# Retention in a two-layer diffusion backbone: rotated queries loaded in three groups instead of chunk by chunk

## The chip, the cores and the metric

The kernel runs on one core of a Trainium2 chip. The metric is the device time of one execution in microseconds (us). Engines are named as the profile names them: PE is TensorE (matmuls), PEld its weight loads, DVE is VectorE, ACT is ScalarE, POOL is GpSimd, SP is the SyncE queue, which issues every load and store spoken of here. All data is float32.

## The reference, cut to what matters

Two layers work on 1024 latent tokens behind 256 context tokens, width 1024. Each layer projects its tokens into three groups of heads (retention, latent attention, grouped attention), joins their outputs in one projection and ends with a gated MLP. The change lies in retention: 6 heads of 64, chunks of 128 tokens, both directions.

```python
def retention_scan(q, k, v, log_gamma, state0):          # chunks of c = 128 tokens
    scores = jnp.einsum('bhncd,bhnsd->bhncs', qc, kc) * decay_mask[None, :, None]
    intra = jnp.einsum('bhncs,bhnse->bhnce', scores, vc)
    kv = jnp.einsum('bhnsd,bhnse->bhnde', kc * k_decay[None, :, None, :, None], vc)
    def step(state, kv_n):
        return chunk_decay[None, :, None, None] * state + kv_n, state
    _, states_prev = lax.scan(step, state0.astype(dt), jnp.moveaxis(kv, 2, 0))
    cross = jnp.einsum('bhncd,nbhde->bhnce', qc * q_decay[None, :, None, :, None], states_prev)
    return (intra + cross).reshape(b, h, t, dv)

def bidir_retention(q, k, v, log_decay, state_fwd, state_bwd):
    out_f = retention_scan(q, k, v, log_decay[0], state_fwd)
    out_b = flip_t(retention_scan(flip_t(q), flip_t(k), flip_t(v), log_decay[1], state_bwd))
    return out_f + out_b

def retention_out(o, g, gn_w):                           # per head: centre, divide by the root of the variance, gate
    ...
```

`q` here is the query after the axial rotation. The product `qc * q_decay` is made on the chip for both directions; it is the tile `qd` below.

## The kernel before, in words

A layer runs one stage after another: input projection, retention, attention, output projection, MLP. The stages are blocks with no overlap between them. The order of the work on each engine is written out by hand, and semaphores carry the waits between engines. The input projection leaves rotated queries, keys, values and gates of retention in a scratch tensor in HBM (`proj`); keys and values are also kept on the chip.

The function `retention` (L1051) has two parts.

**State part.** For each of the 10 chunks PE turns keys and values to token order (`to_tokens`, L1155 and L1162), ACT copies them into `kz` and `vz`, DVE makes the decayed values `vd` from `vz` (L1318), PE multiplies `kz` and `vd` into one state increment (L1176) and counts it in `kv_done`. ACT keeps the increment, DVE scans the states (`scan`, L1325 and L1327). `kz` and `vd` have two slots each and nobody reads them after the last increment, `kv_done` = 10. During this part SP loads the zero-padded queries `qz` (L1111), the first two chunks of `rq` and `gate` (L1115, L1116), and the first head of the attention stage (`fetch_head`, L766 to L769). `rq` holds the same rotated queries as `qz`, unpadded, in two slots of one chunk.

**Chunk loop.** It runs over the chunks of `order`: 10 in the first layer, 8 (without the context) in the last. In iteration i PE does, in this order, `inner(i)` (keys times queries, L1188), `variance(i - 2)` (L1214), `outer(i - 1)` (12 matmuls: L1203 masked scores times values, L1206 `qd` times state), `spread(i - 2)` (L1222). Two more iterations without an `inner` end it. DVE does `masked(i)` (L1352), `invert(i - 2)` (L1358, L1361), one step of the backward scan, `finish(i - 2)` (L1366, L1371), which counts `out_done`. ACT does the roots, the square of the output (L1283) and the block diagonal state (L1276). POOL makes `qd` for both directions, two products of 128x384 for each chunk (L1146), and is busy with nothing else in the loop.

The waits that bear on the change:

```python
pe.wait_ge(at_done, i + 1)       # outer(i): masked scores of chunk i
pe.wait_ge(bd_done, 2 * (i + 1)) #           diagonal states of chunk i
pe.wait_ge(qd_done, 2 * (i + 1)) #           decayed queries of chunk i
if i >= 2: pe.wait_ge(out_done, i - 1)   #   finish(i - 2) has read the output bank
```

On POOL, `qd(i)` waits for the load of `rq(i)` and, from chunk 2 on, for `outer(i - 2)` (`main_done`), which has read the slot of `qd`. On SP, the loads of `rq(i + 2)` and `gate(i + 2)` wait for `out_done` of chunk i, that is for `finish(i)`, and for `qd(i)`; the store of chunk i follows them.

Of the kernel before, what the change touches and what calls it, by code (L numbers as in the profile page):

```python
# [14 lines left out]
P = 128  # L15
KB = D // P
BLK = TOK // P
# [10 lines left out]
T_RK, T_RV, T_RQ, T_RG = (x - RK for x in (RK, RV, RQ, RG))  # L28
# [21 lines left out]
def backbone(nc, a):  # L50
    f32, f32r = mybir.dt.float32, mybir.dt.float32r
    ALU, ACT, AX = mybir.AluOpType, mybir.ActivationFunctionType, mybir.AxisListType
# [4 lines left out]
    def scratch(name, shape):  # L57
        return nc.dram_tensor(f"{name}_scratch", shape, f32, kind="Internal").ap()
    proj = scratch("proj", (NTILE - RK, P, TOK))
# [702 lines left out]
    def fetch_head(sp, h, q0, q1, q2, k1, k2, sem):  # L762

        rows = slice((h % 2) * HD, (h % 2 + 1) * HD)
        for part, q, k in ((0, q1, k1), (1, q2, k2)):
            sp.dma_start(k[:HD, :].bitcast(f32), mk_d[part, h // 2, rows, :]).then_inc(sem, 16)  # L766
            sp.dma_start(k[HD:MD, :].bitcast(f32), kr_d[part]).then_inc(sem, 16)
            sp.dma_start(q[:HD, q0:].bitcast(f32), mq_d[part, h // 2, rows, q0:]).then_inc(sem, 16)
            sp.dma_start(q[HD:MD, q0:].bitcast(f32), mq_d[part, 2, h * MR:(h + 1) * MR, q0:]).then_inc(sem, 16)  # L769
# [281 lines left out]
    def retention(layer, last, first_head):  # L1051
        W = RH * HD
        back = list(range(XB - 1, -1, -1)) + list(range(BLK - 1, XB - 1, -1))
        order = back[XB:] if last else back
        NO = len(order)
        q0 = CTX if last else 0
        with Scope() as s:
# [3 lines left out]
            cdec = s.sb("cdec", [P, 3, 2])  # L1061
            decq = s.sb("decq", [P, 2, 3, P])
            mask, mtmp = s.sb("mask", [P, RH, P]), s.sb("mtmp", [P, RH, P])
            rq, gate = s.sb("rq", [P, 2, 3, P]), s.sb("gate", [P, 2, 3, P])
            qz = s.sb("qz", [P, 3, 2, TOK])
            kz = s.sb("kz", [P, 2, 3, 2 * P])
            vz = s.sb("vz", [P, BLK, 3, 2 * P])
            vd = s.sb("vd", [P, 2, 3, 2, 2, HD])
            kv = s.sb("kv", [P, BLK, 3, 2, HD])
            state = s.sb("state", [P, BLK, 3, 2, HD])  # L1070
            bd = s.sb("bd", [P, 2, 3, 2, P])
            qd = s.sb("qd", [P, 2, 2, 3, P])
# [7 lines left out]
            pa = [s.ps(f"pa{i}", [P, 1024]) for i in range(2)]  # L1080
            po = psum_banks(s, "po", 2)
            mats_in, qz_in, head_in = s.sem("mats_in"), s.sem("qz_in"), s.sem("head_in")
            rq_in = [s.sem(f"rq_in{k}") for k in range(2)]
            gate_in = [s.sem(f"gate_in{k}") for k in range(2)]
            kz_zero, vz_zero, bd_zero, qz_zero = s.sem("kz_zero"), s.sem("vz_zero"), s.sem("bd_zero"), s.sem("qz_zero")
            arg, dec_made, masks_made, mask_made, decq_made = (s.sem(x) for x in ("arg", "dec_made", "masks_made", "mask_made", "decq_made"))
# [1 line left out]
            vd_done, kv_done, kv_kept = s.sem("vd_done"), s.sem("kv_done"), s.sem("kv_kept")  # L1088
            own, fwd_done, bwd_done = s.sem("own"), s.sem("fwd_done"), s.sem("bwd_done")
            a_done, at_done, main_done, bd_done, qd_done = (s.sem(x) for x in ("a_done", "at_done", "main_done", "bd_done", "qd_done"))  # L1090
# [2 lines left out]
            out_stored = [s.sem(f"out_stored{k}") for k in range(2)]  # L1093
            block = s.enter_context(nc.Block())
            halves = [slice(0, HD), slice(HD, P)]

            def own_columns(x, half):

                return x[:, :, half * (P + HD):half * (P + HD) + HD]
# [4 lines left out]
            @block.sync  # L1104
            def _(sp):
                sp.dma_start(centre[:, :], a["ret_centre"]).then_inc(mats_in, 16)
                sp.dma_start(og[:, :], a["ones_gqa"]).then_inc(mats_in, 16)
                c0 = q0
                sp.wait_ge(qz_zero, 2)
                for half in range(2):  # L1110
                    sp.dma_start(qz[halves[half], :, half, c0:], proj[T_RQ:T_RQ + 3, halves[half], c0:].rearrange("t p n -> p t n")).then_inc(qz_in, 16)  # L1111

                def load_chunk(i):
                    c = order[i]
                    sp.dma_start(rq[:, i % 2, :, :], proj[T_RQ:T_RQ + 3, :, c * P:(c + 1) * P].rearrange("t p n -> p t n")).then_inc(rq_in[i % 2], 16)  # L1115
                    sp.dma_start(gate[:, i % 2, :, :], proj[T_RG:T_RG + 3, :, c * P:(c + 1) * P].rearrange("t p n -> p t n")).then_inc(gate_in[i % 2], 16)  # L1116
                load_chunk(0)
                load_chunk(1)
                fetch_head(sp, 0, q0, *first_head, head_in)
                for i, c in enumerate(order):  # L1120
                    sp.wait_ge(out_done, i + 1)
                    if i + 2 < NO:
                        sp.wait_ge(qd_done, 2 * (i + 1))
                        load_chunk(i + 2)
                    sp.dma_start(mix[O_RET:O_RET + 3, :, c * P:(c + 1) * P].rearrange("t p n -> p t n"),
                                 tout[:, i % 2, :].rearrange("p (t n) -> p t n", t=3)).then_inc(out_stored[i % 2], 16)
                for k in range(2):
                    sp.wait_ge(out_stored[k], 16 * (NO // 2))
                sp.wait_ge(head_in, 128)

            @block.gpsimd
            def _(pool):
                nc.gpsimd.memset(kz[:, :, :, HD:P + HD], 0.0).then_inc(kz_zero, 1)
                for half in range(2):
                    pool.wait_ge(qz_zero if half else kz_zero, 1)
                    nc.gpsimd.memset(qz[halves[1 - half], :, half, :], 0.0).then_inc(qz_zero, 1)
                pool.wait_ge(qz_zero, 2)
                nc.gpsimd.memset(vz[:, :, :, HD:P + HD], 0.0).then_inc(vz_zero, 1)
                nc.gpsimd.memset(bd[:, :, :, :, :], 0.0).then_inc(bd_zero, 1)
                pool.wait_ge(decq_made, 6)  # L1140
                for i, c in enumerate(order):
                    pool.wait_ge(rq_in[i % 2], 16 * (i // 2 + 1))
                    if i >= 2:
                        pool.wait_ge(main_done, i - 1)
                    for d in range(2):
                        nc.gpsimd.tensor_tensor(qd[:, i % 2, d, :, :], rq[:, i % 2, :, :], decq[:, d, :, :], ALU.mult).then_inc(qd_done, 1)  # L1146

            @block.tensor
            def _(pe):
# [602 lines left out]
    with main:  # L1752
        first_modulations()
        clear_semaphores()
        for layer in range(DEPTH):
            last = layer == DEPTH - 1
            input_projection(layer, last)
            with Scope() as s:
                first_head = [s.sb(x, [P, TOK], f32r) for x in ("first_qh", "first_ql", "first_kh", "first_kl")]
                retention(layer, last, first_head)  # L1760
                attention(layer, last, first_head)
            output_projection(layer, last)
            mlp(layer, last)

            clear_semaphores()
        final_norm()
# [111 lines left out]
```

## Time and profile before

The median of three runs is 3946.09 us (3945.66 to 3949.57). The profiled execution spans 3941.5 us from its first to its last instruction; the profile gives no other time of that execution.

| | |
|---|---|
| span of the profiled execution | 3941.5 us |
| mean granted TensorE clock | 0.956 |
| PE busy | 3540.9 us, 90% |
| DVE busy | 2487.8 us, 63% |
| ACT busy | 1250.1 us, 32% |
| POOL busy | 669.9 us, 17% |
| HBM traffic | 77 GB/s over the span |
| retention, first layer | from 489.5 to 632.2 us of the span |
| retention, last layer | up to 2652.9 us |

Busy time is the time in which an engine executes; a wait is not busy. The granted clock is a share of TensorE's full speed: 1.00 is its upper level, 2.4 GHz, and 0.50 its lower level, 1.2 GHz. A timeline row gives start, duration, engine, line, operation, output and inputs, how many instructions it merges, and in brackets how long the engine stood idle before it and what released it. A float32 matmul stands as two instructions in these counts, so the 12 matmuls of `outer` are 24.

### The profile page before, as it was taken

The numbers are of one execution on the slowest core, as the hardware profiler recorded it, in microseconds if no ns is written. First come the engines' busy times: TensorE is split into PE (matmuls) and PEld (weight loads), VectorE is DVE, ScalarE is ACT, GpSimd is POOL, SyncE is SP. The second block draws the span as 40 slices with busy tenths as digits, with TensorE's granted clock in tenths as the row PEclk, the third lists the DMA queues.
The fourth block names the chain that finished last, engine by engine and source line by source line (L and its number), as shares of the span: only waits on it lengthen the run. The fifth ranks groups of instructions, "written<-read, shape, count | busy, mean of one in ns | idle before, by whom it ended". The sixth has DMA issues, their size and how long they took to land. (4 is left out here: it accounts for less than half of the span.)

```text
span 3941.5 us, 49189 instructions
## 1 busy us (share of the span) xinstructions
PE 3540.9 (90%) x18524; PEld 2974.4 (75%) x18524; DVE 2487.8 (63%) x3355; ACT 1250.1 (32%) x2126; POOL 669.9 (17%) x284
## 2 busy tenths in 40 slices
PE   2899977999698999999998899869997799999996
PEld 2687776888576888888887577769996577777774
DVE  5655544677427999998866523437784366666666
ACT  1432133667313112111121432316673222222222
POOL 0111120000111222232221111210001132222331
PEclk9899988999899999999999899979998899999998
DMA  5235335121201122112110323424112111111111
GB/s 189 93 120 194 146 78 169 41 50 38 102 19 59 64 77 82 64 65 90 43 33 16 119 94 135 153 66 140 47 36 91 33 48 38 42 48 48 48 48 43
DMA packets 97226, 306.58 MB, mean 78 GB/s; under 512 B 11840, under 2 KB 40384, under 8 KB 95296
## 3 DMA queue, kind: packets, MB, share of 16 engines
q1 hardware_dynamic: 97088, 304.69, 23.6%
q8 instruction: 93, 1.52, 0.2%
q14 instruction: 45, 0.37, 0.0%
HBM read 240.29 MB, written 64.36 MB: 77 GB/s over the span
## 5 line engine op out<-in xcount | busy, mean ns | idle before, releaser
L117 POOL TENSOR_TENSOR wlo<-raw,whi 128x1024 fp32r<-128x1024 f32 x190 | 490.0, 2596 | 1787.1 <-ACT whi L106 1787.0
L145 PE MATMUL up_acc<-h_hi,whi 128*128 128x512 f32 (+1 forms) x1760 | 654.7, 372 | 37.6 <-POOL wlo L117 18.6
L1672 DVE SCALAR_TENSOR_TENSOR xT<-down_acc,mod,xT 128x512 f32<-128x512 f32 (+1 forms) x880 | 562.2, 696 | 177.6 <-PE down_acc L147 174.7
L146 PE MATMUL up_acc<-h_lo,whi 128*128 128x512 f32 (+1 forms) x1760 | 649.9, 369 | 0.0
L147 PE MATMUL up_acc<-h_hi,wlo 128*128 128x512 f32 (+1 forms) x1760 | 649.3, 369 | 0.0
L106 ACT ACTIVATE whi<-raw 128x1024 fp32r<-128x1024 f32 x190 | 200.0, 1056 | 763.6 <-PE down_acc L147 351.0
L145 PEld LDWEIGHTS up_acc<-h_hi,whi 128*128 128x128 f32 x1760 | 333.1, 189 | 103.6 <-ACT up L1599 45.3
L147 PEld LDWEIGHTS up_acc<-h_hi,wlo 128*128 128x128 f32 x1760 | 332.8, 189 | 56.3
L146 PEld LDWEIGHTS up_acc<-h_lo,whi 128*128 128x128 f32 x1760 | 333.2, 189 | 54.2 <-issue 0.2
L145 PE MATMUL proj_acc<-h_hi,whi 128*128 128x512 f32 (+1 forms) x920 | 343.0, 373 | 28.3 <-DVE h_lo L353 15.5
L145 PE MATMUL down_acc<-hid_hi,whi 128*128 128x512 f32 (+1 forms) x880 | 333.1, 379 | 19.9 <-POOL hid_lo L1525 19.9
L1011 DVE TENSOR_REDUCE negmax<-scores 128x1 f32<-128x1280 f32 (+1 forms) x180 | 247.0, 1372 | 162.0 <-PE scores L902 162.0
L146 PE MATMUL proj_acc<-h_lo,whi 128*128 128x512 f32 (+1 forms) x920 | 336.7, 366 | 0.0
L147 PE MATMUL proj_acc<-h_hi,wlo 128*128 128x512 f32 (+1 forms) x920 | 336.3, 366 | 0.0
L147 PE MATMUL down_acc<-hid_hi,wlo 128*128 128x512 f32 (+1 forms) x880 | 330.5, 376 | 0.0
L146 PE MATMUL down_acc<-hid_lo,whi 128*128 128x512 f32 (+1 forms) x880 | 328.7, 374 | 0.0
L206 DVE SCALAR_TENSOR_TENSOR mod_acc<-norm_buf,cs,mod_acc 128x384 f32<-128x384 f32 x364 | 325.8, 965 | 0.7 <-DVE xT L707 0.7
L1525 POOL TENSOR_TENSOR hid_lo<-y,hid_hi 128x1281 fp32r<-128x1281 f32 (+1 forms) x44 | 120.4, 2737 | 1175.0 <-ACT hid_hi L1610 1175.0
L1599 ACT ACTIVATE up<-up_acc 128x512 f32<-128x512 f32 (+1 forms) x220 | 119.4, 550 | 563.2 <-PE up_acc L147 562.9
L980 ACT ACTIVATE pth<-scores 128x512 fp32r<-128x512 f32 (+1 forms) x500 | 225.9, 522 | 211.9 <-PE scores L912 211.9
L1025 DVE TENSOR_TENSOR ptl<-scores,pth 128x512 fp32r<-128x512 f32 (+1 forms) x500 | 264.9, 583 | 13.7 <-ACT pth L980 13.7
L1651 DVE TENSOR_SCALAR y<-up,convw 128x1281 f32<-128x1281 f32 (+1 forms) x88 | 122.7, 1394 | 203.8 <-ACT up L1599 203.8
(191 smaller groups left out, 5916.4 us busy)
## 6 DMA issues: line engine op xcount, KB each, us to landing
raw<-in_w_mlp SPq DMA_DIRECT2D x132, 512.0 KB, 3.9
norm_buf<-in_w_ada SPq DMA_DIRECT2D x52, 768.0 KB, 4.7
raw<-in_w_proj SPq DMA_DIRECT2D x42, 512.0 KB, 5.7
proj_scratch<-stage SPq DMA_DIRECT2D x18, 640.0 KB, 3.6
xT<-in_xT SPq DMA_DIRECT2D x2, 5120.0 KB, 27.0
ada_raw<-in_w_ada SPq DMA_DIRECT2D x12, 768.0 KB, 4.5
raw<-in_w_mix SPq DMA_DIRECT2D x16, 512.0 KB, 6.2
xT<-proj_scratch SPq DMA_DIRECT2D x4, 1920.0 KB, 8.6
```

The lines of the kernel that those rows point to most:

```text
L106: nc.scalar.activation(self.hi[k][:, :], self.raw[k][:, :], ACT.Copy).then_inc(self.hi_ready, 1)
L117: nc.gpsimd.tensor_tensor(self.lo[k][:, :], self.raw[k][:, :], self.hi[k][:, :].bitcast(f32), ALU.subtract).then_inc(self.lo_ready, 1)
L145: nc.tensor.matmul(out, hi, xhi, start=start, stop=False)
L146: nc.tensor.matmul(out, hi, xlo, start=False, stop=False)
L147: return nc.tensor.matmul(out, lo, xhi, start=False, stop=stop)
L206: ins = nc.vector.scalar_tensor_tensor(at, self.raw[:, kb, :], cs[:, kb, w:w + 1], at, ALU.mult, ALU.add)
L980: nc.scalar.activation(pth[G % 2][:, k0:k1, j * P:(j + 1) * P], S[n % 2][:, k0 * P:k1 * P].rearrange("p (b q) -> p b q", q=P), ACT.Copy).t ...
L1011: nc.vector.tensor_reduce(negmax[:, n:n + 1], S[n % 2][:, :CTX if is_ctx(n) else TOK], AX.X, ALU.max, negate=True).then_inc(max_done, 1)
L1025: nc.vector.tensor_tensor(ptl[G % 2][:, k0:k1, j * P:(j + 1) * P], S[n % 2][:, k0 * P:k1 * P].rearrange("p (b q) -> p b q", q=P), pth[G % ...
L1525: nc.gpsimd.tensor_tensor(hid_lo[:, lo_col:hi_col], y[1][:, lo_col:hi_col], hid_hi[:, lo_col:hi_col].bitcast(f32), ALU.subtract).then_inc( ...
L1651: nc.vector.tensor_scalar(o, u[:, lo_col:hi_col], cw(1), cw(3), ALU.mult, ALU.add).then_inc(tap, 1)
L1672: nc.vector.scalar_tensor_tensor(xs, db[g % DB][:, :w], mod_of(layer, 5, m, c), xs, ALU.mult, ALU.add).then_inc(added, 1)
```

## The change: what it does

The two-slot tile `rq` is gone. The chunks of `order` are split into three groups of 2, 4 and 4 (in the last layer 2, 4 and 2), each of them one run of adjacent columns, and each is loaded by one DMA. The first group has a tile of its own, `rq_first`, of the size that `rq` had. The second goes into the memory of `kz`, the third into the memory of `vd`. SP issues the loads of groups two and three after `fetch_head`, as soon as `kv_done` is 10. In the loop SP loads only the gate of chunk i + 2 after `out_done` of chunk i, and no longer waits for `qd_done` there. POOL waits for the semaphore of the chunk's group and reads the chunk's columns from it; its wait for `main_done` stays.

```diff
-            rq, gate = s.sb("rq", [P, 2, 3, P]), s.sb("gate", [P, 2, 3, P])
+            gate = s.sb("gate", [P, 2, 3, P])
+            rq_first = s.sb("rq_first", [P, 3, 2 * P])
...
+            rq_more = [kz[...] as [P, 3, 512], vd[...] as [P, 3, 512]]
...
+            groups = [(rq_first, order[0:2]), (rq_more[0], order[2:6]), (rq_more[1], order[6:10])]
+            def group_of(i):
+                return 0 if i < 2 else 1 if i < 6 else 2
+            def queries(i):
+                dst, cs_ = groups[group_of(i)]
+                at_ = (order[i] - cs_[-1]) * P
+                return dst[:, :, at_:at_ + P]
...
-                def load_chunk(i):
+                def load_queries(g):
+                    dst, cs_ = groups[g]
+                    sp.dma_start(dst[:, :, :len(cs_) * P],
+                                 proj[T_RQ:T_RQ + 3, :, cs_[-1] * P:(cs_[0] + 1) * P].rearrange("t p n -> p t n")).then_inc(rq_in[g], 16)
+                def load_gate(i):
                     c = order[i]
-                    sp.dma_start(rq[:, i % 2, :, :], proj[T_RQ:T_RQ + 3, :, c * P:(c + 1) * P].rearrange("t p n -> p t n")).then_inc(rq_in[i % 2], 16)
                     sp.dma_start(gate[:, i % 2, :, :], ...)
-                load_chunk(0)
-                load_chunk(1)
+                load_queries(0)
+                load_gate(0)
+                load_gate(1)
                 fetch_head(sp, 0, q0, *first_head, head_in)
+                sp.wait_ge(kv_done, BLK)
+                load_queries(1)
+                load_queries(2)
                 for i, c in enumerate(order):
                     sp.wait_ge(out_done, i + 1)
                     if i + 2 < NO:
-                        sp.wait_ge(qd_done, 2 * (i + 1))
-                        load_chunk(i + 2)
+                        load_gate(i + 2)
...
-                    pool.wait_ge(rq_in[i % 2], 16 * (i // 2 + 1))
+                    pool.wait_ge(rq_in[group_of(i)], 16)
...
-                        nc.gpsimd.tensor_tensor(qd[:, i % 2, d, :, :], rq[:, i % 2, :, :], decq[:, d, :, :], ALU.mult).then_inc(qd_done, 1)
+                        nc.gpsimd.tensor_tensor(qd[:, i % 2, d, :, :], queries(i), decq[:, d, :, :], ALU.mult).then_inc(qd_done, 1)
```

## Rows read from the trace of the kernel before

**Rows 1.** Instructions of tile `qd`, whole program: durations in ns, idle and waits.

```profile
L1146 POOL TENSOR_TENSOR qd<-rq,decq x36: 991/991/1703, 515.9 to 2640.6; 128x384 f32<-128x384 f32 x36
...
  DMA rq<-proj_scratch: 151.5, 14
...
  PE po L1203: 62.4, 14
```

**Rows 2.** Timeline of the first layer's loop, iteration 3: the load and what follows.

```profile
536.23 0.38 SPq L1115 DMA_DIRECT2D rq<-proj_scratch  x1
...
538.96 1.94 POOL L1146 TENSOR_TENSOR qd<-rq,decq 128x384 f32<-128x384 f32 x2 [18.02 <-DMA rq<-proj_scratch]
...
541.16 1.19 PE L1203 MATMUL po<-at,vz 128*128 128x128 f32 x4 [4.36 <-POOL qd L1146]
```

**Rows 3.** Timeline of iteration 2 and of the start of iteration 3.

```profile
529.80 1.46 PE L1188 MATMUL pa<-qz,xT 128*128 128x256 f32 x6
...
531.69 0.69 PE L1203 MATMUL po<-at,vz 128*128 128x128 f32 x4
...
534.45 0.49 PE L1222 MATMUL pv<-ident,wide 128*128 128x128 f32 x3
...
534.77 1.46 PE L1188 MATMUL pa<-qz,xT 128*128 128x256 f32 x6
...
535.05 0.56 DVE L1366 TENSOR_TENSOR mtmp<-pv,gate 128x384 f32<-128x384 f32 x1 [0.60 <-PE pv L1222]
535.64 0.56 DVE L1371 TENSOR_TENSOR tout<-po,mtmp 128x384 f32<-128x384 f32 x1
...
536.27 0.96 DVE L1352 TENSOR_TENSOR at<-pa,mask 128x768 f32<-128x768 f32 x1
```

**Rows 4.** Busy time of each engine by stretch, with granted clock, DMA share and GB/s.

```profile
core 0: us, PE busy (x) PEld busy (x) DVE busy (x) ACT busy (x) POOL busy (x), PEclk, DMA share, GB/s
...
632.40:647.10 14.70, 11.64 (x38) 9.38 (x39) 5.07 (x11) 4.87 (x10) 0.00 (x0) 0.50 0.96 297
...
529.69:534.67 4.98, 4.98 (x42) 4.83 (x41) 2.14 (x5) 3.10 (x6) 0.00 (x0) 1.00 0.00 0
2573.20:2578.17 4.97, 4.97 (x41) 4.82 (x40) 2.14 (x5) 3.21 (x6) 0.00 (x0) 1.00 0.00 0
534.45:625.33 90.88, 55.00 (x308) 53.23 (x307) 23.14 (x51) 12.53 (x30) 15.53 (x16) 0.77 0.18 52
2577.84:2645.99 68.15, 41.08 (x230) 39.73 (x229) 16.82 (x38) 9.17 (x22) 11.64 (x12) 0.77 0.18 53
```

**Rows 5.** Timeline at both ends of the loops: spreads and one finish.

```profile
614.45 0.49 PE L1222 MATMUL pv<-ident,wide 128*128 128x128 f32 x3
...
615.71 0.56 DVE L1371 TENSOR_TENSOR tout<-po,mtmp 128x384 f32<-128x384 f32 x1
...
625.33 0.49 PE L1222 MATMUL pv<-ident,wide 128*128 128x128 f32 x3
...
2577.84 0.49 PE L1222 MATMUL pv<-ident,wide 128*128 128x128 f32 x3
...
2645.99 0.49 PE L1222 MATMUL pv<-ident,wide 128*128 128x128 f32 x3
```

**Rows 6.** Timeline: the last state increment, first layer.

```profile
521.45 2.70 PE L1176 MATMUL pa<-vd,kz 128*128 128x128 f32 x12 [3.98 <-issue]
```

**Rows 7.** DMA issues: KB each, median us from issue to landing.

```profile
xT<-proj_scratch SPq DMA_DIRECT2D x4, 1920.0 KB, 8.6
...
gate<-proj_scratch SPq DMA_DIRECT2D x8, 192.0 KB, 2.8
```

**Rows 8.** Timeline: DVE products while POOL makes the first four `qd`.

```profile
516.09 1.06 DVE L1327 TENSOR_TENSOR state<-state,kv 128x192 f32<-128x192 f32 x1
...
517.18 1.63 DVE L1338 TENSOR_TENSOR mtmp<-mtmp,xT 128x768 f32<-128x768 f32 x1
```

**Rows 9.** The MLP's DVE line that reads PSUM, whole program (min/median/max ns).

```profile
L1672 DVE SCALAR_TENSOR_TENSOR xT<-down_acc,mod,xT x880: 473/751/753, 1266.3 to 3903.7; 128x512 f32<-128x512 f32 x140, 128x256 f32<-128x256 f32 x36
```

More of the change, by code:

```diff
@@ L1068, in retention @@
             vd = s.sb("vd", [P, 2, 3, 2, 2, HD])
+            rq_more = [kz[:, :, :, :].rearrange("p i t n -> p (i t n)").rearrange("p (t n) -> p t n", t=3),
+                       vd[:, :, :, :, :, :].rearrange("p i t h d e -> p (i t h d e)").rearrange("p (t n) -> p t n", t=3)]
             kv = s.sb("kv", [P, BLK, 3, 2, HD])
@@ L1082, in retention @@
             mats_in, qz_in, head_in = s.sem("mats_in"), s.sem("qz_in"), s.sem("head_in")
-            rq_in = [s.sem(f"rq_in{k}") for k in range(2)]
+            rq_in = [s.sem(f"rq_in{k}") for k in range(3)]
             gate_in = [s.sem(f"gate_in{k}") for k in range(2)]
```

## Prediction

> **What bounds the kernel now.** I read the tile view of `qd` first, because the change touches only how its input arrives. POOL stood idle 151.5 us in 14 places until a load of `rq` had landed, and PE in turn stood idle 62.4 us in the same 14 places, ahead of `outer`, until POOL had made `qd` [rows 1]. Fourteen is 8 chunks in the first layer and 6 in the last: every chunk but the first two of each loop. So in the chunk loops PE is the engine that works and the load is what it waits for.
>
> The timeline then shows how one such wait is built. The load of chunk 2 is issued at 536.23, right after `finish(0)`, POOL starts at 538.96, needs 1.94 us for both products, and PE starts `outer(2)` at 541.16 after 4.36 us of idleness [rows 2]. The load waits for `finish(i)` of two chunks earlier, although its bytes have been in HBM since the input projection, so this ring of finish, load, `qd`, outer closes again in every iteration.
>
> Third, the same timeline has one iteration that meets no such wait, because the loads of chunks 0 and 1 were issued early. Iteration 2 goes from `inner(2)` at 529.80 to `inner(3)` at 534.77: 4.97 us [rows 3]. The busy times by stretch say that PE was busy for 4.98 of 4.98 us at a granted clock of 1.00 there, and the last layer has the same, 4.97 of 4.97 us at 1.00 [rows 4]. The iterations behind it run otherwise: from the spread at 534.45 to the spread at 625.33, 8 iterations take 90.88 us (11.4 us each) with PE busy 55.00 us at a mean clock of 0.77; in the last layer 6 take 68.15 us with 41.08 us busy, again at 0.77 [rows 4]. After each wait PE falls to the lower level (1.2 GHz): four instructions of `outer(2)` take 1.19 us, the same four of `outer(1)` took 0.69 us [rows 2, 3]. So the wait costs twice, as idle time and as slow matmuls behind it. This double cost is what I expect to go.
>
> **The chunk loop.** What an iteration costs when `qd` is not late is read directly: 4.97 us, PE without a gap, full clock. I have to ask what is late next at that pace. `outer` has four releasers.
>
> The first is `qd` itself. POOL may start it when `outer(i - 2)` is done, about one iteration and 2 us ahead of `outer(i)`, and needs 1.94 us [rows 2]; it has 5 us to spare. The second is `finish`: in iteration 3 it ends at 535.64 + 0.56 = 536.20 [rows 3]. In iteration 2 `outer` began 531.69 - 529.80 = 1.89 us after `inner`, so in iteration 3 it would begin at 534.77 + 1.89 = 536.66. The reserve is 0.46 us less the time that a semaphore takes. It is small, but there. The third, the masked scores, are made one iteration earlier: `masked(3)` at 536.27 serves iteration 4. The fourth, the diagonal state on ACT, is made as early, and ACT has 3.10 us of work in the 4.98 us stretch, a table load among it [rows 4]. DVE has 2.14 us there without a `finish`, 3.26 us with its two products of 0.56 us [rows 3, 4], so it isn't full either.
>
> The gate of chunk i + 2 is still loaded after `finish(i)` and is used in `finish(i + 2)`, two iterations or 9.9 us later; it lands in 2.8 us [rows 7]. That costs nothing. Its issue, and the store's, move forward by the one issue that is gone from ahead of them, 0.38 us [rows 2]; nobody waits for either.
>
> First layer, from the spread of chunk 0 at 534.45 to that of chunk 8: seven iterations with an `inner` at 4.97 us are 34.8 us. The eighth has no `inner`; there `finish` decides when `outer` starts. From the spread at 614.45 to the end of `tout` at 615.71 + 0.56 are 1.82 us [rows 5], a semaphore is about 0.1 us, and `outer` to the next spread at full clock is 534.45 - 531.69 = 2.76 us [rows 3]: 4.7 us. Together 39.5 us in place of 90.88 us, a gain of 51.4 us. Last layer: 5 x 4.97 + 4.7 = 29.6 us in place of 68.15 us, a gain of 38.6 us. Behind the last spread but one nothing changes: those iterations wait for no `qd`. Sum: 90.0 us.
>
> **The new loads.** Each is 768 KB (384 KB for the third group of the last layer). They are issued when the last state increment is done, at 521.45 + 2.70 = 524.15 [rows 6], an issue is about 0.4 us [rows 2], and up to iteration 3 no other DMA moves in this stretch: 0 GB/s in [rows 4]. For the landing the trace bounds me with 2.8 us for 192 KB and 8.6 us for 1920 KB [rows 7]; by bytes between those, 768 KB is 2.8 + 5.8 x 576/1728 = 4.7 us, an estimate. I take 5 us: landed by 530, when `outer(0)` has not long been done. `outer(2)` wants `qd` at 536.66, thus the load by 534.5. Even 8.6 us (533.2) is early enough. The second and third group share the queue; at twice 8.6 us the third is there by 542, and its first user, `outer(6)`, comes four iterations after `outer(2)`, at 556.5. The cost is nothing, at either bound. SP is blocked until 524.15 by its new wait, but what is queued behind is only the wait for `out_done`, which comes at 536.2. The first group replaces two loads of 192 KB by one of 384 KB at the head of a busy queue; POOL needs it at 515.9, when the masks of `decq` are made [rows 1]. Nothing.
>
> **POOL beside DVE.** This is the one resource that is used differently. Before, POOL worked while DVE had nothing to do; now it starts with the end of an `outer`, and its 1.94 us lie beside `mtmp`, `tout` and `masked`. While POOL made its first four `qd`, a DVE product took 1.06 us that takes 0.36 us elsewhere, and one of 128x768 took 1.63 us [rows 8] against 0.96 us for the product of the same size in [rows 3]: 0.7 us more each. Both read two operands from SBUF. The three that will lie beside POOL read one operand from PSUM. Such a one, the MLP's `xT<-down_acc,mod,xT`, has a median of 751 ns and a maximum of 753 ns over the program, though POOL splits weights in that stage [rows 9]. I take zero, and 0.7 us for each of three products as the other bound.
>
> The Trainium skill speaks to just this: by SBUF — State Buffer, in its section "Who interferes with whom", a DVE instruction with two SBUF inputs contends with a GpSimd instruction that reads SBUF and one of them blocks fully, while one with at most one SBUF input, outside the two-port modes, does not. The trace agrees with both halves, 0.7 us added for the one and 2 ns for the other. By that rule the sum stays at 90 us; a rule that made any DVE work block behind POOL would give the rival below.
>
> **Sum.** The profiled span is 3941.5 us, 4.6 us under the median of the runs shown. 3941.5 - 90.0 = 3851.5 us of span, which is 3856 us on the scale of the median.
>
> **Rivals.**
> A. The wait goes but the clock stays low in part. Then PE keeps its 55.00 + 41.08 = 96.1 us of busy time and only the rest of 90.88 + 68.15 = 159.0 us goes, 62.9 us: 3883 us. For it speaks that the loop's clock is 0.77 now; against it, that both undelayed iterations had 1.00, and that the low level appears only after an idle stretch of 4 us, which is gone. Chance 0.06; some of it may mix with the forecast.
> B. POOL and DVE block each other also with PSUM operands. Three products 0.7 us longer make DVE's iteration 3.26 + 2.1 = 5.4 us, with its small gaps 5.7 us; that is 0.7 us over 4.97, 14 times: 10 us back, and a `finish` 1.4 us later against a reserve of 0.4 us gives 1 us, 14 us back. 3866 to 3870 us. [Rows 9] speak against it. Chance 0.09.
> C. The end of the loop is reached in another state of the clock and the attention stage starts slower. That is the case on the slower side. In the first layer PE runs its first 14.7 us of attention at 0.50 now [rows 4], after 4 us of idleness between the stages, and this idleness stays. A longer slow stretch costs at most half of its length, so it would need some 180 us more of it in both layers together to eat the gain, against the 14.7 us seen. A few us of this are likely either way (the range takes 4); slower than 3954 us has a chance of 0.02.
> D. The change doesn't take the load off the path: group two lands after `outer(2)` is due. Each us past 534.5 costs one, once a layer. If it took 17.2 us, twice the longest landing of [rows 7], it would be there at 541.4 and cost 7 us a layer; no change at all would need 45 us a layer. Chance 0.02 for no measurable change, by this or whatever else.
>
> **How the numbers follow.** About 0.2% (8 us) is what a measurement of this kernel tells from no change. The forecast has 0.81 with 3850 to 3862 us of its own: the iteration may be 0.2 us longer or the reserve of `finish` may fail by 0.2 us (14 x 0.4 = 6 us), and the clock at the start of attention may shift by some us. A's and B's times reach up to 3883; I take the range to 3873, which includes B and leaves A out, and down to 3847. Faster: 0.81 + 0.06 + 0.09 = 0.96. Same 0.02, slower 0.02.
>
> **What would show it.** In the profile after, the waits of POOL for the load of queries are gone in the loop, PE has no idle time ahead of L1203 that ends with `qd`, the spreads are 5.0 us apart, the granted clock of both loops is 1.00, and eight iterations take 39 to 40 us. If they take 5.5 us or more with `mtmp` or `tout` above 0.56 us, B is right; if matmuls of `outer` still come four in 1.1 us, A is. I am wrong at the root if another wait of some us stands ahead of `outer`, the one for `finish` being nearest.

## The result, and the profile after

The changed kernel takes 3852.15 us (3849.47 to 3855.89, four runs) against 3945.88 us before; the ratio is 0.9766 with a 95% interval of 0.9754 to 0.9779. Forecast was 3856 us, range 3847 to 3873. The profiled execution spans 3847.7 us (mean granted clock 0.965), before 3941.5 us (0.956): 93.8 us less, where 90.0 were forecast.

The tile view of `qd` after the change, which answers to [rows 1] (durations in ns, then idle time by what ended it, then who waited for it):

```profile
L1168 POOL TENSOR_TENSOR qd<-kz,decq x16: 992/998/1007, 528.7 to 2532.9; 128x384 f32<-128x384 f32 x16
L1168 POOL TENSOR_TENSOR qd<-vd,decq x12: 996/999/1002, 548.3 to 2542.8; 128x384 f32<-128x384 f32 x12
...
  PE po L1228: 55.0, 14
  ACT decq L1283: 27.3, 2
...
  POOL qd L1168: 55.0, 14
```

No load is left in it: the 14 waits of POOL end with `outer` of two chunks earlier, and the waits of PE for `qd`, 62.4 us in 14 places before, are gone. `qd` reads `kz` and `vd`, where the queries now lie.

Iteration 4 of the first layer; before the change it was one of those that held a wait (timeline; compare [rows 2, 3]):

```profile
538.31 1.96 POOL L1168 TENSOR_TENSOR qd<-kz,decq 128x384 f32<-128x384 f32 x2 [3.02 <-PE po L1228]
538.33 1.46 PE L1210 MATMUL pa<-qz,xT 128*128 128x256 f32 x6
...
538.60 0.56 DVE L1388 TENSOR_TENSOR mtmp<-pv,gate 128x384 f32<-128x384 f32 x1 [1.64 <-PE pv L1244]
539.19 0.56 DVE L1393 TENSOR_TENSOR tout<-po,mtmp 128x384 f32<-128x384 f32 x1
...
539.83 0.96 DVE L1374 TENSOR_TENSOR at<-pa,mask 128x768 f32<-128x768 f32 x1
...
540.22 0.69 PE L1225 MATMUL po<-at,vz 128*128 128x128 f32 x4
...
543.30 1.46 PE L1210 MATMUL pa<-qz,xT 128*128 128x256 f32 x6
```

PE goes from one `inner` to the next in 4.97 us and has no idle time anywhere between. `mtmp`, `tout` and the masked scores keep their 0.56, 0.56 and 0.96 us although POOL works beside them from 538.31 to 540.27. The busy times of the two loops, spread of chunk 0 to last full spread, and of the first 14.7 us of attention, answer to [rows 4]:

```profile
core 0: us, PE busy (x) PEld busy (x) DVE busy (x) ACT busy (x) POOL busy (x), PEclk, DMA share, GB/s
...
533.03:572.56 39.53, 38.88 (x309) 37.51 (x308) 23.13 (x52) 12.55 (x30) 13.70 (x14) 1.00 0.28 81
2521.68:2551.26 29.58, 28.93 (x230) 27.87 (x229) 16.82 (x37) 9.18 (x22) 9.80 (x10) 1.00 0.28 81
579.70:594.40 14.70, 11.72 (x39) 9.47 (x39) 5.10 (x10) 4.88 (x11) 0.00 (x0) 0.50 0.97 303
```

Eight iterations take 39.53 us in place of 90.88, six take 29.58 in place of 68.15, both at a clock of 1.00 in place of 0.77. PE's own busy time in the two loops fell from 96.1 to 67.8 us for the same matmuls: that is the clock. The rest of the gain is idle time of PE: 159.0 - 96.1 = 62.9 us in the two loops before, 69.1 - 67.8 = 1.3 us after. Attention starts as slowly as before.

The new loads, from the DMA view of 500 to 560 us (KB each, us from issue to landing):

```profile
gate<-proj_scratch SPq DMA_DIRECT2D x6, 192.0 KB, 2.7
...
kz<-proj_scratch SPq DMA_DIRECT2D x1, 768.0 KB, 4.5
vd<-proj_scratch SPq DMA_DIRECT2D x1, 768.0 KB, 6.3
```

In the experiments below I compare, beside whole times, the time of the two retention stages: from the issue of their first load to the first DVE instruction of attention. It is 142.75 + 120.61 = 263.4 us before and 91.04 + 81.53 = 172.6 us after, a gain of 90.8 us. What lies outside is the same code in all kernels, and over the thirteen profiled executions it varies from 3675.1 to 3680.6 us. The changed kernel's stages took 172.6, 173.0 and 173.2 us in three executions. So the stage view resolves a microsecond, the whole time some 3 to 5.

### The profile page after: what moved, and what is told of

It reads as the page before. It is cut to its first block and busy times, and to the rows that moved or that the text cites. A ratio compares the mean times of both kernels' runs of the same rounds, so it can differ in the third digit from the quotient of the medians.

```text
span 3847.7 us, 49163 instructions
## 1 busy us (share of the span) xinstructions
PE 3509.0 (91%) x18524; PEld 2945.0 (77%) x18524; DVE 2496.8 (65%) x3355; ACT 1250.9 (33%) x2126; POOL 666.3 (17%) x284
## 5 line engine op out<-in xcount | busy, mean ns | idle before, releaser
L1694 DVE SCALAR_TENSOR_TENSOR xT<-down_acc,mod,xT 128x512 f32<-128x512 f32 (+1 forms) x880 | 562.3, 695 | 166.9 <-PE down_acc L147 164.0
L206 DVE SCALAR_TENSOR_TENSOR mod_acc<-norm_buf,cs,mod_acc 128x384 f32<-128x384 f32 x364 | 336.5, 995 | 0.7 <-DVE xT L707 0.6
```

The source lines that it names most:

```text
L206: ins = nc.vector.scalar_tensor_tensor(at, self.raw[:, kb, :], cs[:, kb, w:w + 1], at, ALU.mult, ALU.add)
L1694: nc.vector.scalar_tensor_tensor(xs, db[g % DB][:, :w], mod_of(layer, 5, m, c), xs, ALU.mult, ALU.add).then_inc(added, 1)
```

## Experiments

All ratios are to the kernel before, run on the same chip.

**1. Keep the wait, fill it with work.** The kernel before, with eight matmuls ahead of the wait for `qd`.

```diff
                     pe.wait_ge(bd_done, 2 * (i + 1))
+                    if i >= 2:
+                        for _ in range(8):
+                            nc.tensor.matmul(pa[i % 2][:, 768:1024], rk[:, 0, c * P:(c + 1) * P],
+                                             qz[:, 0, :, c * P:(c + 1) * P], start=True, stop=True)
                     pe.wait_ge(qd_done, 2 * (i + 1))
```

Expected: 

> The kernel before, with eight matmuls of inner's shape (128x256, into columns of the score bank that nobody reads) put ahead of the wait for qd in outer, from chunk 2 on. The wait stays; only what PE does in it changes. My theory says that the wait costs twice, 62.4 us of idleness and about 27.6 us through the low clock in the matmuls behind it. Then the fill takes 8 x 0.43 = 3.4 us of the 4.36 us idle, outer takes 2.7 in place of 3.6 to 5.1 us, the loop's clock is 1.00, the spreads are about 9.4 to 9.7 us apart (11.4 before), and the kernel takes 3946 - 27 = 3919 us. Rival: the slow matmuls are not due to the idleness but to something that comes with the reload, such as its DMA; then the clock stays at 0.77 and the kernel takes 3946 us or, if the slow fill overruns the wait, more.

Measured: 3917.8 us, ratio 0.9939 (0.9923 to 0.9956); retention 130.28 + 109.25 = 239.5 us, 23.8 less than before. The expected 3919 us was counted from 3946 us, 27 us less; on this chip the kernel before takes 3940.4 us, so the whole time fell by 22.6 us. Timeline of iteration 3: the load, the fill (L1198), and `outer` behind it.

```profile
536.03 0.38 SPq L1115 DMA_DIRECT2D rq<-proj_scratch  x1
...
536.47 3.70 PE L1198 MATMUL pa<-qz,xT 128*128 128x256 f32 x16
...
538.73 1.95 POOL L1146 TENSOR_TENSOR qd<-rq,decq 128x384 f32<-128x384 f32 x2 [19.13 <-DMA rq<-proj_scratch]
...
540.73 0.71 PE L1207 MATMUL po<-at,vz 128*128 128x128 f32 x4 [0.56 <-POOL qd L1146]
```

The load, `qd` and the start of `outer` are within 0.5 us of where they were, but four instructions of `outer` take 0.71 us where [rows 2] has 1.19. The undisturbed iterations are 9.2 to 9.4 us long against 11.4 us, and the clock from 534.45 to 613 us is 0.98. So added work makes the kernel faster, by 2.1 us an iteration, and that part of each wait is the clock alone. Two iterations are longer, 13.24 and 10.47 us: there POOL starts 5.1 and 3.9 us after the issue of its load (545.29 to 550.34, 2613.24 to 2617.09), against 2.7 us in the rows above. Those loads landed late, and that is why the sum is 23.8 and not 14 x 2.1 = 29 us. What delayed them is open.

**2. Move the reload one step, leave all else.** The kernel before; the load of `rq` for chunk i + 2 goes ahead of the wait for `out_done`. `load_chunk` is split for it into `load_queries`, the load of `rq`, and `load_gate`; each still serves one chunk.

```diff
...
-                    sp.wait_ge(out_done, i + 1)
                     if i + 2 < NO:
                         sp.wait_ge(qd_done, 2 * (i + 1))
-                        load_chunk(i + 2)
+                        load_queries(i + 2)
+                    sp.wait_ge(out_done, i + 1)
+                    if i + 2 < NO:
+                        load_gate(i + 2)
```

Expected: 

> The kernel before with one edit on SP: the load of the queries of chunk i + 2 is issued once qd of chunk i is made, ahead of the wait for out_done of chunk i instead of behind it. Two slots, one DMA for each chunk, kz and vd untouched. If only the place of the load in the ring costs time, it comes one iteration earlier, about 10 us before outer needs it against the 5 us that load and product take, and the kernel is as fast as the changed one: 3852 us, iteration 4.97 us, clock 1.00. Rival: fewer and larger DMAs, or an SP that issues less in the loop, carry a part of the gain; then this kernel lies above 3852 us by that part, at 3860 us or more, with an iteration over 5.1 us.

Measured: 3873.41 us, ratio 0.9827 (0.9811 to 0.9843), retention 99.4 + 93.8 = 193.2 us. My expectation missed: by its numbers this is what the rival said, 3860 us or more and iterations over 5.1 us, and only experiment 3 tells the two apart. Most of the gain is there, but the first layer's spreads are 4.97, 6.32, 4.97, 6.27, 5.02, 6.32, 4.99 and 8.99 us apart. The timeline shows why the iterations of 6.3 us are longer:

```profile
534.44 0.56 DVE L1378 TENSOR_TENSOR tout<-po,mtmp 128x384 f32<-128x384 f32 x1
...
535.02 0.38 SPq L1119 DMA_DIRECT2D gate<-proj_scratch  x1
...
535.44 0.49 SPq L1132 DMA_DIRECT2D mix_scratch<-tout  x1
...
535.98 0.49 SPq L1115 DMA_DIRECT2D rq<-proj_scratch  x1
...
539.58 1.95 POOL L1153 TENSOR_TENSOR qd<-rq,decq 128x384 f32<-128x384 f32 x2 [8.71 <-DMA rq<-proj_scratch]
...
541.78 0.68 PE L1210 MATMUL po<-at,vz 128*128 128x128 f32 x4 [1.21 <-POOL qd L1153]
```

The load for chunk 3 still stands behind `finish(0)` in SP's queue, and behind two issues more. I had counted 10 us from there to `outer(3)`; `finish(i)` runs at the start of iteration i + 3, so it is 5.4 us, against 6.8 us for issues, landing and product. The 8.99 us belong to the iteration without an `inner`, 4.72 us in the changed kernel: PE stood idle 2.16 us ahead of its `outer`, whose matmuls then ran at the low clock (1.19 us for the first four). In the last layer two iterations take 9.83 and 10.18 us; POOL started on the loads of their chunks 5.4 and 4.9 us after the issue.

**3. Move it two steps.** As before, but SP issues the load of chunk i + 3 when `qd(i + 1)` is made, ahead of the wait for `out_done` of chunk i.

```diff
...
                 fetch_head(sp, 0, q0, *first_head, head_in)
+                sp.wait_ge(qd_done, 2)
+                load_queries(2)
                 for i, c in enumerate(order):
+                    if i + 3 < NO:
+                        sp.wait_ge(qd_done, 2 * (i + 2))
+                        load_queries(i + 3)
                     sp.wait_ge(out_done, i + 1)
                     if i + 2 < NO:
-                        sp.wait_ge(qd_done, 2 * (i + 1))
-                        load_chunk(i + 2)
+                        load_gate(i + 2)
```

Expected: 

> The kernel before with its two slots and one load for each chunk, but SP issues the load of chunk i + 3 as soon as qd of chunk i + 1 is made, before it waits for out_done of chunk i. The run with the load one step earlier gave spreads 4.97 and 6.3 us apart in turn, because the load still stood behind finish of three chunks earlier and behind the issues of a gate and a store. Theory (only the place of the load in the ring costs time): every load is now issued about 9 us before outer needs it, against 6.7 us of issue, landing and product; all spreads are 4.97 us apart and the kernel is within 0.1% of the changed one, ratio 0.976 to 0.978. Rival (grouped loads into dead memory carry a part of it, by fewer DMAs or a free SP): iterations above 5.1 us and a ratio of 0.980 or more.

Beside it on the same chip ran the changed kernel once more: 

> The changed kernel once more, unedited, beside the kernel before on the same chip as the two kernels that follow, so that they can be compared without a difference between chips. Ratio to the kernel before 0.9766 as in its first measurement, within its interval of 0.9754 to 0.9779.

Measured: 3854.83 us, ratio 0.9775 (0.9762 to 0.9788); its neighbour, the changed kernel, 3852.58 us, 0.9766 (0.9752 to 0.9779). Retention takes 173.4 us against 173.2 us of the neighbour, and all full iterations of both layers are 4.97 or 4.98 us. Two slots, one load for each chunk, `kz` and `vd` left alone, twelve DMAs more: the two stages are the same to 0.3 us. POOL still waits for a load in 10 places, 34.8 us in all, but PE no longer waits for `qd` anywhere. The gain is the place of the load in the ring; neither fewer DMAs nor an SP that issues less has a part in it that shows. Whole tiles in dead memory are one way to put it there.

**4. Put one wait back in each layer.** The changed kernel; the two large loads wait for `out_done` of chunk 0.

```diff
-                sp.wait_ge(kv_done, BLK)
-                load_queries(1)
-                load_queries(2)
                 for i, c in enumerate(order):
                     sp.wait_ge(out_done, i + 1)
+                    if i == 0:
+                        load_queries(1)
+                        load_queries(2)
```

(The run kept the wait for `kv_done`, which is over by then.)

Expected: 

> The changed kernel, but the loads of groups two and three wait for out_done of chunk 0, so that exactly one wait a layer is left, that of outer(2), for a load of 768 KB instead of 192 KB. The changed kernel's trace shows this load to land in 4.5 us against 2.6 us. One wait of before cost 11.4 - 4.97 = 6.4 us. Theory (each wait costs its idleness and the clock behind it): idleness 4.4 + 1.9 = 6.3 us and 2 us of low clock, 8.3 us a layer, 16.6 us in all: 3868 to 3869 us, all other iterations at 4.97 us. Rival: the low clock lasts on into later iterations, since a dense loop doesn't bring it back at once; then the next iterations are over 5.5 us as well and the kernel takes 3875 us or more.

Measured: 3872.11 us, ratio 0.9827 (0.981 to 0.9843); retention 99.38 + 91.19 = 190.6 us, 18.0 more than in the changed kernel (16.6 expected; the whole time says 20 us by the medians and 24 by the ratios, both uncertain by some us). Timeline of iteration 3 in the first layer:

```profile
535.89 0.38 SPq L1130 DMA_DIRECT2D kz<-proj_scratch  x1
...
540.61 3.85 POOL L1169 TENSOR_TENSOR qd<-kz,decq 128x384 f32<-128x384 f32 x4 [21.08 <-DMA kz<-proj_scratch]
542.81 1.19 PE L1226 MATMUL po<-at,vz 128*128 128x128 f32 x4 [6.40 <-POOL qd L1169]
...
546.22 0.61 PE L1226 MATMUL po<-at,vz 128*128 128x128 f32 x4
```

6.40 us of idleness, and four instructions take 1.19 us; at 546.22 they take 0.61 us again. This iteration is 13.05 us long; the full ones behind it are 4.97 us. In the last layer PE waits 6.70 us, the low clock lasts to the end of that `outer`, and the iteration takes 14.31 us; the next takes 5.11 us, those behind it 4.97 us. The rival, a low clock that lasts over several iterations, is refuted: one wait costs its own iteration and at most 0.14 us of the next, 8.3 us in the first layer and 9.7 in the last.

**5. Put products with two SBUF operands beside POOL.** The changed kernel; from chunk 2 on the step of the backward scan stands between the two products of `finish`.

```diff
-                def finish(i):
+                def finish(i, j):
...
                                             gate[:, i % 2, :, :], ALU.mult).then_inc(on_done, 1)
+                    if j < BLK:
+                        backward(j)
```

Expected: 

> The changed kernel with DVE's step of the backward scan moved, from chunk 2 on, between the two products of finish, where POOL is making qd. The scan's two products read two operands from SBUF. If those contend with POOL (0.36 us became 1.06 us for one of them in the state part) and the ones with an operand in PSUM do not, the two scan products take about 1.06 us each or up to 1 us of waiting each, mtmp, tout and the masked scores stay at 0.56, 0.56 and 0.96 us, tout ends 1.6 to 2.1 us later, 1.2 to 1.8 us past the reserve of finish, and iterations grow to 6.2 to 6.8 us: 12 such iterations, 15 to 22 us, 3867 to 3874 us. Rival: no contention in this place; the scan takes 0.72 us, tout is late by 0.75 us against a reserve of 0.46 us, 0.3 to 0.4 us an iteration, 4 to 5 us: 3856 to 3857 us.

Measured: 3868.0 us, ratio 0.9817 (0.98 to 0.9833); retention 189.1 us, 16.5 more than the changed kernel; iterations of 6.20 to 6.27 us, the theory's case. Timeline of iteration 3:

```profile
534.67 2.07 POOL L1168 TENSOR_TENSOR qd<-kz,decq 128x384 f32<-128x384 f32 x2 [2.68 <-PE po L1228]
...
534.95 0.56 DVE L1388 TENSOR_TENSOR mtmp<-pv,gate 128x384 f32<-128x384 f32 x1 [1.26 <-PE pv L1244]
535.43 0.46 DVE L1347 TENSOR_TENSOR state<-state,cdec 128x192 f32<-128x192 f32 x1
535.92 1.03 DVE L1349 TENSOR_TENSOR state<-state,kv 128x192 f32<-128x192 f32 x1
...
537.10 0.56 DVE L1395 TENSOR_TENSOR tout<-po,mtmp 128x384 f32<-128x384 f32 x1
...
537.80 0.68 PE L1225 MATMUL po<-at,vz 128*128 128x128 f32 x4 [1.09 <-DVE tout L1395]
```

The scan's second product takes 1.03 us in place of 0.36, `mtmp` beside the same POOL work keeps its 0.56 us. `tout` ends at 537.66, 3.30 us after the spread's start at 534.36, where it was 1.75 us in [rows 3]; 1.55 us later costs this iteration 1.23 us, and where `tout` ends 1.62 us later it costs 1.30 us, so the reserve of `finish` was 0.32 us. Not all of the 16.5 us is contention: undelayed, the two scan products would still make `tout` some 0.75 us late, which by this reserve is 0.43 us in each of 12 iterations, some 5 us (an estimate). The other 11 us or so are.

**6. Take POOL off the state part.** The changed kernel still has the idleness of [rows 6] ahead of the last state increment (3.99 us now), with four `qd` of POOL beside DVE's products from SBUF [rows 8]. These four take 5.00 us; in experiment 4, beside no such product, four take 3.85 us. Timeline of the changed kernel:

```profile
514.60 5.00 POOL L1168 TENSOR_TENSOR qd<-rq_first,decq 128x384 f32<-128x384 f32 x4 [14.08 <-ACT decq L1283]
```

I made three variants of POOL's first two chunks:

```diff
                 pool.wait_ge(decq_made, 6)
+                pool.wait_ge(vd_done, BLK)          # variants a and b
...
+                    if i == 1:
+                        pool.wait_ge(at_done, 1)    # variants b and c
```

Expected for a, only the first wait: 

> The changed kernel with one more wait: POOL begins its first qd only when the last decayed values of the state part are made. In the state part four qd beside DVE's products with two SBUF operands delay these by 0.70, 0.67 and 1.47 us, PE stands idle for 3.99 us ahead of the last state increment and works at the low clock for some 5 us behind it, in both layers. Theory: the last increment starts 2.8 us earlier, PE's idle time there falls to about 1.2 us, the clock stays at 1.00 and saves another 2 us: 4 to 5 us a layer, 8 to 10 us in all, ratio 0.974 to 0.9745. Rival: POOL's work now lies beside the mask sum and the scans, which delays the first masked scores, or qd of chunk 0 is late for outer(0); then it gives back as much and the ratio stays at 0.9766.

Expected for b, both: 

> The changed kernel with POOL's first qd (two products) after the last decayed values, and its second only after the first masked scores. In the run that only waited for the decayed values all four products lay beside the scans and the mask sum (1.05, 1.64, 1.04 and 1.03 us in place of 0.36, 0.96, 0.35 and 0.36), PE stood idle 2.26 us ahead of the first outer and nothing was gained. Theory (the conflict is one of POOL's and DVE's products with SBUF operands and its sum is what counts): now two products meet DVE's, about 1.4 us of delay instead of 2.8, the second qd lies beside products from PSUM; outer(0) starts 1.4 to 3 us earlier than in the changed kernel, 3 to 6 us in all, ratio 0.975 to 0.976. Rival: PE falls to the low clock at the last wait that is left, and what is gained in waits goes there; ratio 0.9766 or more.

Expected for c, only the second: 

> The changed kernel with its first qd where it is, at once when the decay tables are made, and the second only after the first masked scores. Two of DVE's products in the state part are delayed instead of four: the last decayed values come about 1.5 us earlier, PE's idle time ahead of the last state increment falls from 3.99 to about 2.5 us, and nothing else is late. Theory: 1.5 us a layer and perhaps 1 us of low clock, 3 to 5 us in all, ratio 0.9755 to 0.976, about as good as the kernel that goes with it. Rival as there: 0.9766.

Measured: a 3852.05 us, 0.9768 (0.9755 to 0.9781), retention 173.2 us; b 3843.39 us, 0.9752 (0.9739 to 0.9766), 167.0 us; c 3849.57 us, 0.9757 (0.9744 to 0.977), 169.9 us. In a the last increment does come earlier, but POOL's four products then meet the scans and the mask sum:

```profile
518.29 1.58 PE L1199 MATMUL pa<-vd,kz 128*128 128x128 f32 x12 [1.14 <-issue]
518.33 4.81 POOL L1169 TENSOR_TENSOR qd<-rq_first,decq 128x384 f32<-128x384 f32 x4 [17.15 <-DVE vd L1341]
518.49 1.05 DVE L1350 TENSOR_TENSOR state<-state,kv 128x192 f32<-128x192 f32 x1
519.57 1.64 DVE L1364 TENSOR_TENSOR mask<-mask,mtmp 128x768 f32<-128x768 f32 x1
...
524.71 1.20 PE L1226 MATMUL po<-at,vz 128*128 128x128 f32 x4 [2.26 <-DVE at L1375]
```

PE's 3.98 us of idleness became 1.14 and 2.26 us, and `outer` runs at the low clock (1.20 us for four): nothing gained, the rival's case. In b the second `qd` waits, and the same two places read:

```profile
516.86 1.57 PE L1201 MATMUL pa<-vd,kz 128*128 128x128 f32 x12 [1.14 <-issue]
516.90 2.07 POOL L1171 TENSOR_TENSOR qd<-rq_first,decq 128x384 f32<-128x384 f32 x2 [16.79 <-DVE vd L1343]
...
521.93 0.68 PE L1228 MATMUL po<-at,vz 128*128 128x128 f32 x4 [0.90 <-DVE at L1377]
```

In c PE's idleness ahead of the last increment is 2.52 us, where 2.5 were expected, and the stages are some 3 us shorter than in the changed kernel: half of what b gains.

Since b was the best, I ran it again beside the changed kernel. Expected for b: 

> The kernel with the first qd after the last decayed values and the second after the first masked scores, once more, beside the changed kernel on one chip. Its first measurement gave 0.9752 (0.9739 to 0.9766) where the changed kernel has 0.9766. If the 3 to 6 us are real, its median lies 3 to 6 us below its neighbour's; if they were the spread of repeated runs, within 2 us of it.

Expected for its neighbour: 

> The changed kernel, unedited, as the neighbour on the same chip of the kernel with the split first qd. Ratio 0.9766, within 0.9754 to 0.9779.

Measured: b 3846.98 us, 0.9749 (0.9736 to 0.9763), retention 166.9 us; the changed kernel 3850.43 us, 0.9761 (0.9748 to 0.9775), 173.0 us. The two stages are shorter by 5.6 to 6.3 us in both executions of b, and its median is 3.5 us below its neighbour's. The intervals of the whole time overlap, so b is shown better in its stage and only probably so in the whole.

## Why the prediction was right

- **The wait costs twice.** Right, and shown apart: experiment 1 takes away only the clock part, 2.1 us an iteration or 29 us in all, and PE's busy time in the loops fell by 96.1 - 67.8 = 28.3 us. The rest of the gain, 90.8 - 29 = about 62 us, is the idleness, which [rows 1] had as 62.4 us. Rival A needed the clock to stay low; it is 1.00.
- **The iteration that was undisturbed before is the iteration after.** 4.97 us read, 4.97 us measured, in both layers. The last iteration was put at 4.7 us and is 4.72 us. The two loops gained 51.35 + 38.57 = 89.9 us against 51.4 + 38.6.
- **What is late next.** `finish` was named as the nearest, with 0.46 us less a semaphore; experiment 5 measured 0.32 us. It never decides in the full iterations of the changed kernel. In the one without an `inner` it does, as forecast.
- **The new loads cost nothing.** Put at 4.7 us by the two landings of [rows 7], measured 4.5 us. POOL started on them when `outer(0)` ended, not when they landed. Experiment 4 shows what a late one would have cost: 8 to 10 us a layer. Rival D fell. One step was thinner than it reads: the 0 GB/s of [rows 4] cover 529.69 to 534.67 us, and the load is under way before that; from 524.15 to 529.69 the trace has 3 GB/s, so the conclusion holds.
- **POOL beside DVE.** Right in its result: nothing for the three products with an operand in PSUM. But the evidence for it was misread. No one of the 880 products of [rows 9] ran beside work of POOL: POOL's last split ahead of them ended at 1265.01 us, the first of them started at 1266.34, and none comes nearer to work of POOL than 1.1 us. Their 751 and 753 ns say nothing of contention. So the rows bore out the 0.7 us for two SBUF operands and not yet the zero for one; what was left for the zero, and for the small chance of rival B, was the rule of the Trainium skill, and that this piece of evidence pointed the right way was luck. The trace had a better row, the products of the output projection, which read PSUM too:

```profile
L1454 DVE SCALAR_TENSOR_TENSOR xT<-out_acc,mod,xT x40: 483/751/752, 1052.2 to 3101.0; 128x512 f32<-128x512 f32 x32, 128x256 f32<-128x256 f32 x8
```

  Five of its eight short ones lie whole within a product of POOL of 2.40 us (the first at 1067.00, POOL from 1065.27) and take 484 to 485 ns, against 483 to 484 for the three others. The profile after settles it for the products of the loop. Rival B fell, and experiment 5 shows its mechanism alive one operand away: the same loop with the scan's two products in this place, both operands in SBUF, gives back 16.5 us, some 11 of them by contention. The Trainium skill's rule (SBUF — State Buffer, section "Who interferes with whom") is that a DVE instruction with two SBUF inputs contends with a GpSimd one that reads SBUF. It foretold which products would be hit, and these runs agree: 0.36 us became 1.03, while `mtmp` kept its 0.56.
- **The start of attention.** Rival C fell: 14.7 us at 0.50 before and after.
- **The remaining 3.0 us** of the 93.8 lie outside retention, where unchanged code varies by 5.5 us from execution to execution. I take them for that; no run singles them out.

## What to carry to other kernels

When a loop's first iterations run without a wait because their loads were issued early, read their length: here it was what the loop cost once the load was off the ring, clock included. It needs no model, but it has to be asked what will then run side by side that did not before, and a row that is to show such a pair harmless must be one in which both really run at the same time. A wait of some 4 us in every iteration cost half as much again here through the clock of the matmuls behind it, and even useless work in its place made the kernel faster. And before giving a reload new memory, look where its issue stands in the queue: moved ahead of a wait for the end of the pipeline, the same two slots gave the same time, but it has to be counted in iterations where that wait really ends.

## What the runs showed of the hardware

- POOL's products and DVE's products with two SBUF operands delay each other, and either engine can be the one that loses. Beside POOL's products of 1.0 us a DVE product lost 0.7 us, whether short or long (0.36 to 1.05 us, 0.96 to 1.64 us). POOL lost little beside short ones (two products in 2.07 us in place of 1.95) and more beside long ones: four took 5.00 us in the changed kernel and 4.81 us in variant a, in place of 3.85, and the longest single one took 1703 ns where the median is 991 [rows 1]. The loss was larger beside a longer product: at 442.51 us of the kernel before, beside a product of POOL of 2.40 us, a DVE product of 128x1024 took 3.10 us, where its median is 1.23.
- A DVE copy from SBUF to SBUF is hit too. In experiment 3 POOL's start drifted until it lay beside the copy that spreads the roots (timeline):

```profile
546.86 2.06 POOL L1155 TENSOR_TENSOR qd<-rq,decq 128x384 f32<-128x384 f32 x2 [4.49 <-DMA rq<-proj_scratch]
546.98 1.10 DVE L1370 COPY wide<-root 128x384 f32<-128x384 f32 x1
```

  It took 1.10 us in place of 0.36, and the iteration stayed at 4.97 us: the copy ended at 548.08 us, and the spread that reads it came only at 549.03, behind `outer`.
- The low clock lasted for different times. Behind the wait of 6.40 us in experiment 4 the four matmul instructions at 542.81 us take 1.19 us and those at 546.22 take 0.61; behind the wait of 6.70 us in its last layer the clock was 0.50 from 2540.7 to 2545.9 us, with PE busy throughout. At the start of attention, behind 4 us of idleness, PE stayed at 0.50 for 14.7 us although it was busy for 11.7 of them.
- Waits of half the length of those in the kernel before were followed by the low clock too: 2.16 us in experiment 2 (5.3 us at 0.50 behind it) and 2.26 us in variant a. Behind 1.21 us (experiment 2) and 0.90 us (variant b) the four matmul instructions took 0.68 us.
